# A two-layer hybrid trunk: six groups of the gate's product go between index scores, two stores change their queue, weights are exchanged at other key tiles

## What is computed

```python
proj = xn @ w_in
a_u, a_v, b_q, b_k, b_v, i_q, i_k, i_w = split(proj)
a_out = gmlp_spatial_gate(gelu(a_u), gelu(a_v), w_s, b_s, ln_g, ln_b)
b_out = dsa_attention(b_q, b_k, b_v, i_q, i_k, i_w, rel_bias)
mix = concatenate([a_out, b_out]) @ w_out
```

## Time and profile before

| what | us |
|---|---|
| median of three runs | 2519.82 |
| the profiled execution | 2515.06 |
| its span, first to last instruction | 2512.8 |
| TensorE matmul busy | 2407.7 (96%) |
| VectorE busy | 1700.9 (68%) |
| ScalarE (ACT) busy | 1182.8 (47%) |
| GpSimd (POOL) busy | 1471.1 (59%) |
| mean granted TensorE clock | 0.986 |

### The profile page before, as it was taken

How to read it: one execution, slowest core, us unless ns; L and a number is a source line. 1 busy time by engine, 2 the same in 40 slices (tenths; PEclk the granted TensorE clock), 3 DMA queues, 4 the chain that set the end, 5 groups by cost and what they waited for, 6 DMA issues and landing times.

```text
span 2512.8 us, 34098 instructions
## 1 busy us (share of the span) xinstructions
PE 2407.7 (96%) x11680; PEld 1985.4 (79%) x11680; DVE 1700.9 (68%) x2859; ACT 1182.8 (47%) x2025; POOL 1471.1 (59%) x813
## 2 busy tenths in 40 slices
PE   7899999998998999999999999989999999999997
PEld 6689888776876878888778887878777888778886
DVE  5469999676775596555656677167787565666676
ACT  5442633566664374444333336165665444433331
POOL 2111578655553149877678642456637888577951
PEclk9999999999999999999999999989999999999999
DMA  5390544833645624554644444756553545754343
GB/s 148 67 133 26 127 105 138 252 102 92 177 122 168 230 70 144 166 153 151 238 168 157 144 134 135 173 135 175 143 191 101 157 140 166 246 184 150 102 143 133
DMA packets 330515, 369.63 MB, mean 147 GB/s; under 512 B 14002, under 2 KB 229586, under 8 KB 328324
## 3 DMA queue, kind: packets, MB, share of 16 engines
q1 hardware_dynamic: 321748, 351.96, 48.0%
q10 hardware_dynamic: 8352, 15.21, 2.0%
q0 software_dynamic: 272, 0.62, 0.1%
HBM read 237.18 MB, written 130.55 MB: 146 GB/s over the span
## 4 chain that ended last, share of the span: by engine, by line
PE 66%; DVE 6%; ACT 4%; issue 3%; DMA 2%; SPq 0%; POOL 0%; DVEq 0%; ACTq 0%; POOLq 0%
PE ps L468 62%; PE ps L2757 2%; PE ps L2836 1%; DMA h_operand_raw<-h_operand_scratch 1%; ACT logits L1706 1%; PE ps L2766 1%; DVE logits L2273 1%; DVE acc L1957 1%; DVE probs_T L2308 1%; ACT probs_T L1731 1%; ACT junk L1389 1%; DVE acc L1976 0%; PE ps L2846 0%; DVE xn_T L2060 0%; ACT xn_T L1425 0%
## 5 line engine op out<-in xcount | busy, mean ns | idle before, releaser
L468 PE MATMUL ps<-xn_T,w_split 128*128 128x512 f32 (+1 forms) x2928 | 677.5, 390 | 2.2 <-ACT x_sums L1433 2.0
L468 PEld LDWEIGHTS ps<-xn_T,w_split 128*128 128x128 f32 (+1 forms) x2928 | 547.2, 187 | 120.1 <-DVE xn_T L2060 2.5
L468 PE MATMUL ps<-w_operand,h_operand 128*128 128x512 f32 x2016 | 463.6, 392 | 13.4 <-DVE acc L2542 6.7
L468 PEld LDWEIGHTS ps<-w_operand,h_operand 128*128 128x128 f32 x2016 | 381.1, 189 | 95.8 <-issue 13.0
L423 POOL TENSOR_TENSOR w_split<-w_raw,w_split 128x1024 fp32r<-128x1024 f32 x74 | 189.0, 2564 | 448.4 <-ACT w_split L416 448.1
L1303 POOL TENSOR_TENSOR w_split<-w_raw,w_split 128x512 fp32r<-128x512 f32 x168 | 244.3, 1467 | 102.0 <-ACT w_split L1821 100.6
L468 PE MATMUL ps<-x_sums_high,w_split 128*128 128x512 f32 x896 | 284.9, 389 | 0.0
L2544 DVE TENSOR_TENSOR acc<-acc,ps 128x512 f32<-128x512 f32 x288 | 185.8, 680 | 130.4 <-PE ps L468 129.9
L1335 POOL TENSOR_TENSOR w_operand<-w_block,w_operand 128x2048 fp32r<-128x2048 f32 x42 | 207.3, 4937 | 109.7 <-ACT w_operand L1841 109.7
L1828 ACT ACTIVATE h_operand<-h_operand_raw 128x2048 fp32r<-128x2048 f32 (+1 forms) x56 | 95.3, 1702 | 262.8 <-DMA h_operand_raw<-h_operand_scratch 262.8
L2474 DVE TENSOR_TENSOR h_operand<-h_operand_raw,h_operand 128x2048 fp32r<-128x2048 f32 (+1 forms) x56 | 164.8, 2944 | 56.6 <-ACT h_operand L1828 56.5
(11 more groups left out here) (284 smaller groups left out, 4256.5 us busy)
## 6 DMA issues: line engine op xcount, KB each, us to landing
h_operand_raw<-h_operand_scratch SPq DMA_DIRECT2D x42, 1024.0 KB, 5.1
w_raw<-in_w SPq DMA_DIRECT2D x72, 512.0 KB, 8.1
w_block<-in_w SPq DMA_DIRECT2D x48, 512.0 KB, 6.1
q_scratch<-q_split SPq DMA_DIRECT2D x128, 128.0 KB, 2.6
cat_scratch<-attn_out_split SPq DMA_DIRECT2D x128, 128.0 KB, 2.6
w_raw<-in_w_in SPq DMA_DIRECT2D x30, 512.0 KB, 5.1
q_tile<-q_scratch ACTq DMA_DIRECT2D x58, 256.0 KB, 2.7
unit_tile<-cat_scratch SPq DMA_DIRECT2D x56, 256.0 KB, 4.1
```

The source lines that it names most:

```text
L468: return nc.tensor.matmul(out_ap, stat, mov, start=start, stop=stop)
```

## The change

Six of the 32 groups of the gate half (cp = 0, t = 0 to 5) are run in halves of 12 matmuls behind scores 9, 13, 17, 20, 23, ... 44; ACT takes the gelu of a finished group one score later. The block `gelu_v` gets another layout, so that the first groups' results have a place while scores run. The bias lines lie where the gain rows lie later, their stores are issued by ACT ahead of its first relu, VectorE waits for them no longer, and SP loads the gain rows behind the weight tiles. The normalizer is made two bit steps later. Step (3,6) gets a fill and (3,0) has none; fills 16 and 31 have plans of their own; the eight tiles' high and low parts have new places.

```diff
--- before.py
+++ after.py
@@ -88,6 +88,9 @@
 
 SCORES = [(b + e, h) for b in range(2, NB, 2) for h in range(IDX_HEADS) for e in range(2)]
 
+AV_HALF = {n: divmod(k, 2) for k, n in enumerate((9, 13, 17, 20, 23, 26, 29, 32, 35, 38, 41, 44))}
+AV_TAKE = {n + 1: t for n, (t, half) in AV_HALF.items() if half}
+
 KEYS0 = [b + 1 for b in range(NB)]
 WIDTH1 = [P if b == 0 else P + CHUNK for b in range(NB)]
 STEP1 = [(2 * kv + e, b) for kv in range(2) for b in range(NB) for e in range(2)]
@@ -109,13 +112,15 @@
     steps, k = {}, 2
     for i in range(HG):
         for b in range(NB):
-            n = 2 if (i, b) == (1, 4) else 0 if (i, b) in ((1, 5), (3, 6), (3, 7)) else 1
+            n = 2 if (i, b) == (1, 4) else 0 if (i, b) in ((1, 5), (3, 0), (3, 7)) else 1
             steps[i, b] = list(range(k, k + n))
             k += n
     return steps
 
 
-SWAP_STEP = {1: 5, 3: 6}
+SWAP_HIGH = {(1, 4, "end"): [4], (1, 5, 5): [5], (1, 5, "end"): [6], (1, 6, 5): [7],
+             (3, 6, 5): [8], (3, 6, 6): [9], (3, 7, "end"): [10, 11]}
+SWAP_LOW = {(1, 5): ([4, 5], [6]), (1, 6): ([7], []), (3, 7): ([8, 9], [10, 11])}
 FILL = fill_steps()
 
 
@@ -215,13 +220,13 @@
     wsT = at("w_s_T", [P, 2, GROUPS, P], F32R, D0 + 78 * K)
     oh = at("onehot", [32, 2, REL_SPAN], F32, D0 + 4 * K)
     flag = at("sel_flag", [P, 2, 1024], U8, D0 + 86 * K)
-    lines = at("bias_lines", [48, REL_SPAN], F32, D0 + 86 * K)
+    lines = at("bias_lines", [48, REL_SPAN], F32, 0)
     qraw = at("q_raw", [P, 2, 512], F32, D0 + 18 * K)
     q2eo = at("q_split", [P, 2, 2, 512], F32R, D0 + 22 * K)
-    gv = at("gelu_v", [P, NB, D], F32, D0 + 30 * K)
+    gv = at("gelu_v", [P, 4, 3, NB, 128], F32, D0 + 30 * K)
     bs2 = at("b_s_split", [33, T], F32R, D0 + 26 * K)
-    vln = at("v_ln_split", [P, 2, NB, P], F32R, D0 + 62 * K)
-    gu = at("gate_u", [P, T], F32, D0 + 70 * K)
+    vln = at("v_ln_split", [P, 2, 3, NB, P], F32R, D0 + 38 * K)
+    gu = at("gate_u", [P, T], F32, D0 + 62 * K)
     svs = at("sv_sb", [P, T], F32, D0 + 74 * K)
     aohl = at("a_out_split", [P, 2, T], F32R, D0 + 18 * K)
     q_first = at("q_tile_first", [P, 4, 2, 4, P], F32R, XT0)
@@ -395,7 +400,19 @@
         return aohl_7 if g == 7 else aohl_6 if g == 6 else aohl
 
     def v_ln(g):
-        return vln_7 if g == 7 else vln
+        return vln_7 if g == 7 else vln[:, :, 0]
+
+    def v_block(cp):
+
+        return gv[:, (cp + 3) % 4, 0:2].rearrange("p a b m -> p (a b m)").rearrange("p (t c) -> p t c", t=NB)
+
+    def v_group(g):
+
+        return v_block(g // 2)[:, :, (g % 2) * P:(g % 2 + 1) * P]
+
+    def v_rows(t):
+
+        return gv[:, :, t // 4, 2 * (t % 4):2 * (t % 4) + 2, :]
 
     def gate_in(g):
         return gu_7 if g == 7 else gu
@@ -1031,16 +1048,15 @@
         sp.wait_ge(a_free, A_Q)
         sp.dma_start(k2d, k2st[:].bitcast(F32)).then_inc(kv_sp, 16)
         sp.dma_start(vd, vhl[:].bitcast(F32)).then_inc(kv_sp, 16)
-        for l in range(2):
-            sp.dma_start(lined[l], lines[32 * l:32 * l + HEADS, :].unsqueeze(1).to_broadcast([HEADS, P, REL_SPAN])).then_inc(line_sp, 16)
-        sp.wait_ge(ws_ok, 1)
-        for g in range(4):
-            load_gain(g)
         sp.wait_ge(kv_sp, 32)
         for r in (0, 32):
             sp.dma_start(bsraw[r:r + 1, :], b_s).then_inc(oh_bs_ld, 16)
         for n in range(T_AV + 4, T_Q + 4):
             load_tile(sp, n, tile_src(n))
+        sp.wait_ge(ws_ok, 1)
+        sp.wait_ge(line_sp, 32)
+        for g in range(4):
+            load_gain(g)
         for m in range(8):
             load_tile(sp, T_Q + 4 + m, tile_src(T_Q + 4 + m))
             for f in (2 * m, 2 * m + 1):
...
@@ -1248,11 +1264,11 @@
                 pool.wait_ge(at_ld, 16)
             if g + 3 < HG * NB:
                 mask_bias(g + 3)
-            if i % 2 and b == SWAP_STEP[i]:
-                n = T_O0 + 4 * (i // 2 + 1) + 2
-                split_lo(pool, n)
-                split_lo(pool, n + 1)
-                pool.wait_ge(w_lo, n + 2)
+            ahead, behind = SWAP_LOW.get((i, b), ([], []))
+            for m in ahead:
+                split_lo(pool, T_O0 + m)
+            if ahead:
+                pool.wait_ge(w_lo, T_O0 + ahead[-1] + 1)
             pool.wait_ge(o_ok, g + 1)
             nc.gpsimd.tensor_copy(olo[:, s, :], osb[HD:P, s, :]).then_inc(o_low, 1)
             pool.wait_ge(o_low, g + 1)
@@ -1261,11 +1277,10 @@
             pool.wait_ge(o_rest, g + 1)
             nc.gpsimd.tensor_tensor(ohl[:, s, 1, :], osb[0:HD, s, :], olo[:, s, :], ALU.add).then_inc(ol_ok, 1)
             pool.wait_ge(ol_ok, g + 1)
-            if i % 2 and b == SWAP_STEP[i] - 1:
-                n = T_O0 + 4 * (i // 2 + 1)
-                split_lo(pool, n)
-                split_lo(pool, n + 1)
-                pool.wait_ge(w_lo, n + 2)
+            for m in behind:
+                split_lo(pool, T_O0 + m)
+            if behind:
+                pool.wait_ge(w_lo, T_O0 + behind[-1] + 1)
 
     def pool_attn1(pool):
 
@@ -1552,6 +1567,16 @@
             act.wait_ge(a_full, f + 1)
             nc.scalar.activation(wsT[:, 0, 4 * k:4 * k + 4, :], ps[:, f % 4, :].rearrange("p (g t) -> p g t", g=4), ACT.Copy).then_inc(a_hi, 1)
 
+        def take_value(cp, t):
+
+            f = B_AV + 8 * cp + t
+            act.wait_ge(b_full, f + 1)
+            nc.scalar.activation(v_block(cp)[:, t, :], ps[:, 4 + f % 4, 0:256], ACT.Gelu,
+                                 accum_out=gsum[:, t, cp:cp + 1]).then_inc(b_free, 1)
+
+        act.wait_ge(a_free, A_Q)
+        for l in range(2):
+            act.dma_start(lined[l], lines[32 * l:32 * l + HEADS, :].unsqueeze(1).to_broadcast([HEADS, P, REL_SPAN])).then_inc(line_sp, 16)
         for n in range(len(SCORES)):
             b = SCORES[n][0]
             w = (b + 1) * P
@@ -1561,20 +1586,21 @@
                 act.wait_ge(rl_used, n - 1)
             nc.scalar.activation(rl[:, d, 0:w], ps[:, 2 * d:2 * d + 2, :].rearrange("p a n -> p (a n)")[:, 0:w],
                                  ACT.Relu).then_inc(sc_free, 1)
+            if n in AV_TAKE:
+                act.wait_ge(kv_sp, 32)
+                take_value(0, AV_TAKE[n])
 
         act.wait_ge(rl_used, len(SCORES))
         for cp in range(4):
             split_hi(act, T_AV + 2 * cp + LOOK)
             for t in range(NB):
-                f = B_AV + 8 * cp + t
-                act.wait_ge(b_full, f + 1)
-                nc.scalar.activation(gv[:, t, cp * 256:(cp + 1) * 256], ps[:, 4 + f % 4, 0:256], ACT.Gelu,
-                                     accum_out=gsum[:, t, cp:cp + 1]).then_inc(b_free, 1)
+                if cp or t >= len(AV_TAKE):
+                    take_value(cp, t)
             split_hi(act, T_AV + 2 * cp + 1 + LOOK)
         act.wait_ge(ln_mu, 1)
         act.wait_ge(kv_sp, 32)
         for t in range(NB):
-            link(nc.scalar.activation(gu[:], gv[:, t, :], ACT.Square, bias=negmu[:, t:t + 1], accum_out=sqv[:, t:t + 1]))
+            link(nc.scalar.activation(gu[:].rearrange("p (a b m) -> p a b m", a=4, b=2), v_rows(t), ACT.Square, bias=negmu[:, t:t + 1], accum_out=sqv[:, t:t + 1]))
         nc.scalar.activation(sdv[:], sqv[:], ACT.Sqrt, scale=1.0 / D, bias=epst[:, 0:1]).then_inc(ln_sq, 1)
 
         for m in range(8):
...
@@ -1731,8 +1757,8 @@
                 nc.scalar.activation(pT[:, x % 4, 0, :], ps[:, 4 + y % 2, :], ACT.Copy).then_inc(c_hi, 1)
                 if todo and st >= 1:
                     exps(g + 1, todo.pop(0))
-                if i % 2 and b == SWAP_STEP[i] and 1 <= st <= 4:
-                    split_hi(act, T_O0 + 4 * (i // 2 + 1) + st - 1)
+                for m in SWAP_HIGH.get((i, b, st), []):
+                    split_hi(act, T_O0 + m)
                 if g and st == min(2, KEYS0[b] - 1):
                     out_high(g - 1)
             act.wait_ge(d_full, g + 1)
@@ -1741,10 +1767,14 @@
             nc.scalar.activation(rec[:, g % 2, :], ps[:, 4 + (X0[g] + g + KEYS0[b]) % 2, :], ACT.Copy).then_inc(d_free, 1)
             for j in todo:
                 exps(g + 1, j)
+            if g == 0:
+                act.wait_ge(ao_lo, GROUPS - 1)
             if g + 5 < HG * NB:
                 load_q(act, qst, g + 5, g + 5)
             if not more:
                 out_high(g)
+            for m in SWAP_HIGH.get((i, b, "end"), []):
+                split_hi(act, T_O0 + m)
 
     def act_attn1(act, first_tiles):
 
@@ -2172,7 +2202,6 @@
             dve.wait_ge(tk, n)
             nc.vector.tensor_scalar(row(b), row(b), MASKED, None, ALU.mult, ALU.add, accum_out=unused).then_inc(mask_ok, 1)
 
-        dve.wait_ge(line_sp, 32)
         dve.wait_ge(v_ch, chain[0])
         bounds = tick(nc.vector.memset(bound[:], 0))
         for bit in range(31, -1, -1):
@@ -2186,7 +2215,7 @@
                 bounds = tick(nc.vector.scalar_tensor_tensor(bound[:], bound[:], 1 << (bit - 1), turn[:], ALU.bitwise_xor, ALU.bitwise_xor))
             else:
                 bounds = tick(nc.vector.tensor_tensor(bound[:], bound[:], turn[:], ALU.bitwise_xor))
```

(53 more changed lines are left out.)

## The result

| | kernel before | changed kernel |
|---|---|---|
| median, runs of one chip (5 each) | 2518.41 us (2516.15 to 2527.75) | 2527.70 us (2524.37 to 2530.36) |
| ratio | 1 | 1.0032, 95% interval 1.0020 to 1.0044 |
| profiled execution, its span | 2515.06, 2512.8 us | 2524.37, 2522.0 us |
| mean granted clock | 0.986 | 0.984 |

By the ratio the change costs 0.3%, some 8 us; the two medians differ by 9.3 us and the spans of the profiled executions by 9.2. The forecast was +0.9, or 2520.7: the range (2506 to 2533) held, but the median lies 7 us above the forecast and just above the range that the main case gave itself (2514 to 2527).

A forecast was written before the change was run, and what follows sets the result against it. It took TensorE to bound the stage windows, the relu round trip and VectorE the score stage before. -17.3 + 13.1 + 7.5 + 1.0 - 3.4 = +0.9 us gave 2520.7, range 2506 to 2533.

The forecast's parts named there:

- the main case: All terms together give +0.9 us, 2520.7; own range 2514 to 2527, chance 0.45.
- part 2: Line stores moved to ACT's queue ahead of the first relu: ACT held, first relu 7.5 us later, +7.5.
- The clock term of 1.0: Before the first relu: with nothing to do until 112 us, TensorE's full clock comes back later, +1.0 (0 to 3).
- Part 1: Six gate product groups moved among the index scores: -17.3 us in the product, +13.1 in the score stage.
- VectorE off the path: Selection starts with the last score, not waiting for the lines; its 10.3 us of slack stay: no gain, no loss.
- not held by the lines: SP, freed of the line stores, loads weight tiles 10 to 12 during the score stage: no effect on time.
- Part 3: Splits and fills moved in the attention steps: (1,5), (3,6), (3,0), (3,7) shorter, (1,6) +5.1 by a wait; sum -3.4 us.
- ACT not held: Rival: ACT's two line issues take 0.8 us, relus start as now; -7.6, 2512.2 us, chance 0.25.
- Idle time takes the halves: Rival: TensorE's idle time in the score stage absorbs the halves, stage growth 1 to 6; 2508 to 2514 us, chance 0.12.
- No wait in (1,6): Rival: TensorE doesn't wait for POOL's low parts in attention step (1,6); 2515.6 us, chance 0.05.
- Table reloads: Rival: each gelu among relus reloads ACT's table, 12 x 1.28 = 15.4 us; 2536 us, chance 0.05.
- The long hold: Rival: ACT is held 37.5 us by the line stores, first relu at 141.8; 2550 us, chance 0.08.

The follow-up runs named there:

- lines_sp: The changed kernel with both line stores back on SP behind K and V, their new home kept; 2513.2 us, ratio 0.9981.
- quarters: lines_sp with the same six groups of the gate product in 24 quarters of 6 matmuls instead of 12 halves; 2507.2 us, ratio 0.9942.
- tiles_first: quarters with the next three weight tiles loaded by SP behind K and V, ahead of the two line stores; 2506.4 us, ratio 0.9939.
- tiles_first_exchange: tiles_first with tiles 5 and 6 split one key tile earlier in step (1,5), tile 7 at its end; 2504.8 us, ratio 0.9930.

## Why the prediction was nearly right, and where it was not

- **The step that failed is the size of the hold in part 2.** The text took "the row of the same two transfers", 0.94 + 7.60 us, and said that K and V "use the same DMA engines at the same moment", as if that made the two cases equal. It is a large part of what makes them differ. Measured: 16.84 us for both issues instead of 8.54, the first relu 16.5 later instead of 7.5. Of the second issue's 16.1, 6.2 go when K and V aren't under way on the other queue; why 9.95 are left and not 7.6 stays open. The mechanism was right: both issues named, the long one second, the relus behind it, TensorE with nothing else ready.
- The clock term of 1.0: the low level lasted until 128.0 us, 7 us behind the first relu, against 4 us in lines_sp (until about 110.5). The stretch from first relu to product was 60.5 against 60.1 in lines_sp: 0.4. But it was 62.0 and 60.0 in two more executions with the late relu, and 60.0 and 60.3 in two with the early one, so 0.4 is within the scatter.
- **Part 1 was right.** The product lost 17.28 (forecast 17.3). The stage grew by 13.1 in the changed kernel and by 12.7 in lines_sp (forecast 13.1), but not where it was put: by the starts of relus 0, 16, 32 and 47 in lines_sp, 2.8 in blocks 2 and 3 (forecast 1.6), 5.4 in 4 and 5 (5.8), 4.6 in 6 and 7 (5.8). Three scores with a half took 4.5 us and 3.9, against 4.8 and 4.1. Errors of both signs met, so that the sum came within 0.4 is in part luck. The two-deep buffers as the reason are borne out by quarters.
- **VectorE off the path: right, but its slack was not forecast.** The selection starts at 183.2 with no wait. "The 10.3 us of slack stay" was wrong: it is 24.75 us (10.29 before). The selection took 250.2 us instead of 262.7: 4.4 of these were a wait of the normalizer for ACT (std_v), which went with the move by two bits, and about 8 came from small operations of 6 columns that ran shorter in this execution (sel_turn 19.3 us in all instead of 24.9, sel_bound 12.6 instead of 14.8).
- SP "not held by the lines" was wrong as well: it was held 21.9 us at a weight tile. It cost nothing.
- **Part 3 was right to 0.5 us:** (1,5) -2.8 (forecast -3.3), (3,6) -3.2 (-3.0), (3,0) -1.9 (-1.8), (3,7) -0.8 (-1.2 + 0.8), (1,6) +5.3 (+5.1), and 0.2 in (3,1) that was not seen. Rounded as they are, they add to -3.2; from the last product of (1,4) to that of (3,7) the changed kernel's lag falls from 12.4 to 9.4 us, net -3.1 against -3.4.
- Together, from rows: 16.9 (late relu and clock) - 17.3 + 12.7 - 3.1 = +9.2; the spans differ by 9.2.
- Rivals. ACT not held: false. Idle time takes the halves: false for halves, half true for quarters. No wait in (1,6): false. Table reloads: false; the rows show one load of 1.28 us ahead of the first gelu, and a relu right behind a gelu at 136.34 with none. By the Trainium skill (ScalarE: Activation LUTs, section on table sets) relu is in every set; the trace agrees. The long hold lay nearer than its chance of 0.08 says: it put 37.5 us on the second issue and took the sign as decided beyond 20; 16.1 came.

## What to carry to other kernels

An issue's price on one queue isn't its price on another: ask what stands ahead of it there, and what drains beside it. Never put two large stores of small pieces in a row on the engine that the next stage waits for; one there and the other behind the stage cost 0.7 and 0.56 us. Work put in the gaps of a round trip should be cut no longer than one operation of the engine that follows (here 0.72 us against relus of 0.7 to 1.0): the same six groups cost the stage 12.7 us as halves and 6.0 as quarters.

## What the runs showed that was not expected

- The hold of the second of two such issues, the same transfers each time: 7.5 to 7.6 us on SP behind K and V, 9.8 and 10.1 on SP behind K, V and three weight tiles (`tiles_first`, `tiles_first_exchange`), 9.95 on ACT alone, 15.9 to 16.1 on ACT with K and V on SP's queue, 0.56 on ACT 62 us later.
- A store on the other queue slows one down that the same store behind it on its own queue doesn't: V landed in 5.0 us with the lines behind it on its queue, in 14.7 to 15.1 with one or both lines on the other, and in 24.0 when it was issued with both lines under way there.
- Moving the lines to ACT's queue didn't free SP's: the third weight tile's issue took 21.9 us there.
- A wait of TensorE for 1 to 3 us can cost more behind it: in (1,6) the granted clock was 0.92 over the window with the waits and 1.00 without them.
